# Banded attention with the keys' low part blanked out to 128 rows for each group

## The chip, the cores and the metric

The kernel runs on one core of one Trainium2 chip. The metric is the device time of the whole kernel in microseconds. A profile is one execution, recorded instruction by instruction.

## The reference, cut to what matters

The reference is two transformer blocks. The part that the change touches is the banded attention of the first block (two layers), over 1024 latent tokens and 256 context tokens, with six query heads in two groups that share keys and values:

```
def block(args):                       # 128 queries, each sees 256 context keys and a band of up to 384
    i, q_b = args
    start = i * Q_BLOCK
    k_b = lax.dynamic_slice_in_dim(kp, start, band, axis=1)
    v_b = lax.dynamic_slice_in_dim(vp, start, band, axis=1)
    q_pos = start + q_off
    k_pos = start - SWA_WINDOW + k_off
    valid = (jnp.abs(q_pos[:, None] - k_pos[None, :]) <= SWA_WINDOW) & ((k_pos >= 0) & (k_pos < s_len))[None, :]
    s_loc = jnp.einsum('bqgrd,bkgd->bgrqk', q_b, k_b).astype(jnp.float32) * SWA_SCALE
    s_loc = jnp.where(valid, s_loc, -jnp.inf)
    s_ctx = jnp.einsum('bqgrd,bcgd->bgrqc', q_b, k_ctx).astype(jnp.float32) * SWA_SCALE
    p = sink_softmax(jnp.concatenate([s_ctx, s_loc], axis=-1), sink).astype(v.dtype)
    return (jnp.einsum('bgrqc,bcgd->bqgrd', p[..., :n_ctx], v_ctx)
            + jnp.einsum('bgrqk,bkgd->bqgrd', p[..., n_ctx:], v_b))
```

Layer 0 also lets the 256 context tokens attend to themselves. The head dimension is 64. Everything is float32.

## The kernel before, in words

The program is a row of stages; each is a block in which every engine has its own instruction stream, and at its end all engines meet in a barrier. `window_attention` is one such stage and runs twice, for layer 0 (with context tokens) and for layer 1 (without). It has no DMA and, before the change, nothing on GpSimd except the clearing of semaphores.

The work is cut into units: one block of 128 queries and one of six heads. Layer 0 has 2 context blocks and 8 latent blocks, so 60 units; layer 1 has 8 latent blocks, 48 units. Context units see 2 tiles of 128 keys, the units of the first and last latent block 4, and all others 5.

The score products are made in a fast format of float32 that keeps only a high part. So queries and keys are each split into a high and a low part. `keys` holds, for each of the two groups, the keys' high part twice: in rows 0 to 63 and again in rows 64 to 127. `qs` holds, for a group, the queries' high part in the group's own 64 rows (`half(g)`) and the low part in the other 64. One matmul with the 128-row tile `q2` over `keys` therefore gives high times high plus low times high. The remaining term, the queries' high part times the keys' low part, is a second matmul (L982) with the 64-row tile `q1`, over `klo`, where both groups share one tile of 128 rows, 64 rows each. Both add into the same bank of PSUM. Masks of the band are added by a matmul of a bf16 identity with a bf16 mask (L984).

TensorE's order is written out by hand: scores of units 0 and 1, and then for each unit u the transposes of its probabilities (`turned`, L993), the scores of unit u + 2 (L981, L982, L984), and the products with the values (`products`, L1003 and L1010). The other engines follow by semaphores:

- ScalarE splits off the high parts (L1031 keys, L1039 queries, once per block), takes the exponentials (L1047, and L1051 for the sink), and copies the first four transposed tiles back (L1064).
- VectorE makes the low parts (L1078 keys, L1085 queries), the row maximum (L1092) and its scaling (L1093), copies the fifth transposed tile (L1119), and makes reciprocal (L1100) and output (L1102). In the loop its order for unit u is: fifth tile of u, maximum of u + 2, output of u - 1, and once in six units the queries of the next block.

The first scores wait for `k_lo` and `q_lo`. `products(u)` waits for the output of u - 2 (`o_out`), the sink's exponential and the copies of the transposed tiles.

Of the kernel before, what the change touches and what calls it, by code (L numbers as in the profile page):

```python
# [8 lines left out]
F32 = mybir.dt.float32  # L9
# [12 lines left out]
NT = NCTX + NLAT  # L22
# [528 lines left out]
class Scaled:  # L551
# [65 lines left out]
    def link(self, dve):  # L617
        if self.linked is None:
            self.linked = Links(dve, self.own)
        return self.linked  # L620
# [214 lines left out]
CKV, KR, SK, SVT, CQ, SQ, CB, CC, CU = 0, 1, 2, 3, 4, 6, 9, 11, 13  # L835
# [86 lines left out]
def window_attention(k, l, with_ctx):  # L922
# [6 lines left out]
    PR, MIX, SV = k.at(PR0, 15, NT), k.at(HT0, KD, NT), k.at(SV0, NT // P * 2, P)  # L929
# [1 line left out]
    prev, nxt, idb = (k.bmask[:, n * P:(n + 1) * P] for n in range(3))  # L931
    NB, H = NLAT // P, 6
    o = XT0
    keys, klo = k.part(o, 2, NT), k.part(o + 2 * NT, NT)
    o += 3 * NT
    qs = [k.part(o + 6 * P * g, 2, 3, P) for g in range(2)]
    o += 12 * P
    sinks, es = k.at(o, H, P), k.at(o + H * P, 2, P)
# [13 lines left out]
    half = lambda g: slice(64 * g, 64 * g + 64)  # L952

    with k.stage() as (block, sem):
        k_hi, k_lo, q_hi, q_lo, s_full, nb_set, p_set, sk_set, own = [sem() for _ in range(9)]
        t_full, pt_a, pt_b, pv_done, r_set, o_out = [sem() for _ in range(6)]
        pieces = ([(0, NCTX), (NCTX, NLAT)] if with_ctx else [(0, NT)])
        piece = lambda u: 2 if units[u][0] and with_ctx else 1

        @block.tensor  # L960
        def _(pe):
            def scores(u):
                kind, b, h = units[u]
                g, f, n = h % 2, h // 2, u // H
                if h == 0:
                    pe.wait_ge(k_lo, 2 * piece(u))
                    pe.wait_ge(q_lo, 2 * n + 2)
                if u >= 2:
                    pe.wait_ge(p_set, u - 1)
                S = k.psum[:, 1024 * (u % 2):1024 * (u % 2) + 1024]  # L970
                q2, q1 = qs[g][:, n % 2, f, :], qs[g][half(g), n % 2, f, :]
                todo = [(0, 0, NCTX, [])]
                if kind:
                    t = band(b)
                    masks = {b - 1: prev, b + 1: nxt}
                    todo += [(NCTX, NCTX + P * t[0], 2 * P, t[:2])]
                    if len(t) > 2:
                        todo += [(512, NCTX + P * t[2], P, t[2:])]
                for c0, k0, n_, ts in todo:
                    hide = [(c0 + P * x, masks[y]) for x, y in enumerate(ts) if y in masks]  # L980
                    pe.matmul(S[:, c0:c0 + n_], q2, keys[:, g, k0:k0 + n_], start=True, stop=False, skip_group_check=True)  # L981
                    mm = pe.matmul(S[:, c0:c0 + n_], q1, klo[half(g), k0:k0 + n_], start=False, stop=not hide, skip_group_check=True)  # L982
                    for c1, mask in hide:
                        mm = pe.matmul(S[:, c1:c1 + P], idb, mask, start=False, stop=True, skip_group_check=True)  # L984
                mm.then_inc(s_full, 1)

            def turned(u):
                pe.wait_ge(p_set, u + 1)
                if u:
                    pe.wait_ge(pt_a, u)  # L990
                    pe.wait_ge(pt_b, second(u)) if second(u) else None
                for t in range(tiles(u)):
                    mm = pe.transpose(k.bank[4 + t // 4][:, (t % 4) * P:(t % 4 + 1) * P], pr[:, u % 2, t * P:(t + 1) * P], k.ident[:, :])  # L993
                    if t == min(4, tiles(u)) - 1 or t == 4:
                        mm.then_inc(t_full, 1)

            def products(u):
                kind, b, h = units[u]
                if u >= 2:
                    pe.wait_ge(o_out, u - 1)  # L1000
                pe.wait_ge(sk_set, u + 1)
                out = k.bank[6 + u % 2][:, 0:P]
                pe.matmul(out, es[:, u % 2, :], k.ident[:, :], start=True, stop=False)  # L1003
                for t in range(tiles(u)):
                    if t == 0:
                        pe.wait_ge(pt_a, u + 1)
                    if t == 4:
                        pe.wait_ge(pt_b, second(u + 1))
                    tile = t if t < CT else CT + band(b)[t - CT]
                    mm = pe.matmul(out, SV[:, 2 * tile + h % 2, :], pt[:, u % 2, t, :], start=False, stop=(t == tiles(u) - 1))  # L1010
                mm.then_inc(pv_done, 1)

            scores(0)
            scores(1)
            for u in range(N):
                turned(u)
                if u + 2 < N:
                    scores(u + 2)
                products(u)

        def count_t(u):

            return u + second(u)

        @block.scalar
        def _(act):
# [43 lines left out]
        @block.vector  # L1070
        def _(dve):
            link = Links(dve, own)

            def keys_of(n):
                t0, nt = pieces[n]
                for g in range(2):
                    dve.wait_ge(k_hi, 2 * n + g + 1)
                    dve.tensor_tensor(klo[half(g), t0:t0 + nt], PR[half(g), SK, t0:t0 + nt], keys[half(g), g, t0:t0 + nt].bitcast(F32),  # L1078
                                      ALU.subtract).then_inc(k_lo, 1)

            def queries(n):
                t0 = tokens(*blocks[n])
                for g in range(2):
                    dve.wait_ge(q_hi, 2 * n + g + 1)
                    dve.tensor_tensor(qs[g][half(1 - g), n % 2, :, :], PR[half(g), SQ:SQ + 3, t0:t0 + P],  # L1085
                                      qs[g][half(g), n % 2, :, :].bitcast(F32), ALU.subtract).then_inc(q_lo, 1)

            def maxima(u):
                h = units[u][2]
                dve.wait_ge(s_full, u + 1)  # L1090
                n = tiles(u) * P
                link(dve.reduce_max(mx[:, u:u + 1], k.psum[:, 1024 * (u % 2):1024 * (u % 2) + n], AX.X))  # L1092
                dve.tensor_scalar(nb[:, u:u + 1], mx[:, u:u + 1], -SWA_SCALE, sink[:, h:h + 1], ALU.mult, ALU.min).then_inc(nb_set, 1)  # L1093

            def outputs(u):
                kind, b, h = units[u]
                t0 = tokens(kind, b)
                out = k.bank[6 + u % 2]
                dve.wait_ge(pv_done, u + 1)
                dve.reciprocal(rec[0:64, u % 2, :], out[64:P, 0:P]).then_inc(r_set, 1)  # L1100
                dve.wait_ge(r_set, u + 1)
                dve.tensor_tensor(MIX[half(h % 2), 3 + h // 2, t0:t0 + P], out[0:64, 0:P], rec[0:64, u % 2, :], ALU.mult).then_inc(o_out, 1)  # L1102

            queries(0)
            keys_of(0)
            link(dve.memset(sinks[:, :, 0:64], -1e30))
            for h in range(H):
                link(dve.tensor_scalar(sinks[:, h, 64:P], k.ones[:, 0:64], sink[:, h:h + 1], -1.0, ALU.mult, ALU.mult))
            maxima(0)
            queries(1)  # L1110
            if len(pieces) > 1:
                keys_of(1)
            maxima(1)
            for u in range(N):
                if tiles(u) > 4:
                    dve.wait_ge(t_full, count_t(u) + 2)
                    if u >= 2:
                        dve.wait_ge(pv_done, u - 1)
                    dve.tensor_copy(pt[:, u % 2, 4, :], k.bank[5][:, 0:P]).then_inc(pt_b, 1)  # L1119
                if u + 2 < N:  # L1120
                    maxima(u + 2)
                if u:
                    outputs(u - 1)
                if u % H == 2 and 2 <= u // H + 1 < len(blocks):
                    queries(u // H + 1)
            outputs(N - 1)
# [693 lines left out]
def first_half(k, l):  # L1820

    with_ctx = l < LAYERS - 1
    project_in(k, l, with_ctx)
    window_attention(k, l, with_ctx)
    latent_projections(k, l, with_ctx)
    latent_attention(k, l, with_ctx)
    mixed(k, l, with_ctx)
    return lambda kt, t0: k.gain[:, (2 * l + 1) * KD + kt, (1 if t0 < NCTX else 0):(2 if t0 < NCTX else 1)]
# [1845 lines left out]
```

## Time and profile before

| | us |
|---|---|
| median of three runs | 4456.78 (4451.52 to 4461.4) |
| span of the profiled execution | 4445.8 |
| stage in layer 0, from the first scores on | 203.31 |
| stage in layer 1, from the first scores on | 174.31 |

The profiled execution has a span of 4445.8 us from its first to its last instruction; its own total time is not listed beside it, so the span stands against the runs, whose median is 11.0 us above. PE is TensorE's matmul, PEld its weight load, DVE VectorE, ACT ScalarE, POOL GpSimd, SP the queue that issues DMAs. PEclk is the share of TensorE's full clock that was granted. The end of a matmul in the trace is modelled and includes its latency, so matmuls overlap in the records; the distance between starts tells the pace. L982 is line 982 of the kernel.

### The profile page before, as it was taken

To read this page: it belongs to the slowest core of one execution; us is meant where nothing else is said; L and a number is where in the kernel's file an instruction comes from. 1 tells how busy PE (TensorE), PEld (TensorE's weight loads), DVE (VectorE), ACT (ScalarE), POOL (GpSimd) and SP (SyncE) were. 2 spreads that over 40 slices of the span, in tenths; PEclk is the share of its full clock that TensorE was granted. 3 is DMA by queue.
4 is the path that set the end of the run, shared out by engine and by line. 5 is a ranking of instruction groups with operands and counts; after the bars stand their busy time and mean duration, and the time that the engine had idled before them with its cause. 6 is when DMAs were issued, how large, how long until landed. Compare 5 with 4: busy or idle time off the path is not lost. (4 is left out here: it accounts for less than half of the span.)

```text
span 4445.8 us, 51677 instructions
## 1 busy us (share of the span) xinstructions
PE 4031.7 (91%) x20694; PEld 3142.7 (71%) x20694; DVE 2167.2 (49%) x3353; ACT 1301.5 (29%) x2259; POOL 506.4 (11%) x597
## 2 busy tenths in 40 slices
PE   7989999897999979898988799799976999998997
PEld 5878655664777769785656699677744778887875
DVE  3577655423111155676553433475565365554444
ACT  3234533222111132344333233311344211112232
POOL 1000111102212210002111111200102100000011
PEclk8999999997999989998999899899887999999999
DMA  6000000337766641000012799312001211112111
GB/s 247 33 20 1 16 1 1 139 155 314 260 249 236 210 173 39 15 1 16 1 67 107 273 337 346 106 48 86 21 1 53 76 43 48 48 48 82 50 57 57
DMA packets 73878, 453.30 MB, mean 102 GB/s; under 512 B 8000, under 2 KB 12624, under 8 KB 57680
## 3 DMA queue, kind: packets, MB, share of 16 engines
q1 hardware_dynamic: 56960, 389.73, 23.2%
q0 software_dynamic: 13088, 47.19, 3.9%
q10 hardware_dynamic: 3632, 13.63, 0.8%
q8 instruction: 138, 2.26, 0.2%
q14 instruction: 60, 0.49, 0.0%
HBM read 394.95 MB, written 55.57 MB: 101 GB/s over the span
## 5 line engine op out<-in xcount | busy, mean ns | idle before, releaser
L2290 PEld LDWEIGHTS psum<-words,words 128*128 128x128 f32 x4096 | 514.6, 192 | 10.4 <-issue 9.1
L2290 PE MATMUL psum<-words,words 128*128 128x160 f32 (+1 forms) x4096 | 515.9, 289 | 1.4 <-DVE words L392 0.9
L675 PE MATMUL psum<-words,words 128*128 128x512 f32 x1104 | 440.6, 399 | 32.3 <-DVE words L715 27.9
L676 PE MATMUL psum<-words,words 128*128 128x512 f32 x1104 | 441.6, 400 | 0.0
L677 PE MATMUL psum<-words,words 128*128 128x512 f32 x1104 | 436.8, 396 | 0.0
L1605 PE MATMUL psum<-words,words 128*128 128x428 f32 (+1 forms) x720 | 253.2, 352 | 29.4 <-DVE words L1698 29.4
L675 PEld LDWEIGHTS psum<-words,words 128*128 128x128 f32 x1104 | 210.9, 191 | 86.3 <-DVE words L715 29.4
L1317 PE MATMUL psum<-words 128*128 128x512 f32 (+1 forms) x504 | 255.1, 588 | 0.0
L1606 PE MATMUL psum<-words,words 128*128 128x428 f32 (+1 forms) x720 | 249.9, 347 | 0.0
L1607 PE MATMUL psum<-words,words 128*128 128x428 f32 (+1 forms) x720 | 249.1, 346 | 0.0
L677 PEld LDWEIGHTS psum<-words,words 128*128 128x128 f32 x1104 | 209.8, 190 | 48.4
L676 PEld LDWEIGHTS psum<-words,words 128*128 128x128 f32 x1104 | 209.9, 190 | 46.9 <-issue 1.0
L694 ACT ACTIVATE words<-words 128x1024 fp32r<-128x1024 f32 x69 | 73.1, 1060 | 579.8 <-DMA words<-in_w_up 379.3
L1361 ACT ACTIVATE words<-psum 128x512 f32<-128x512 f32 (+1 forms) x252 | 147.7, 586 | 293.5 <-PE psum L1309 293.5
L1389 DVE TENSOR_REDUCE words<-psum 128x1 f32<-128x512 f32 (+1 forms) x300 | 163.3, 587 | 143.9 <-PE psum L1287 143.1
L792 PE MATMUL psum<-words,words 128*128 128x512 f32 (+1 forms) x448 | 173.9, 388 | 33.6 <-DVE words L515 33.3
L1307 PE MATMUL psum<-words,words 97*128 97x512 f32 (+1 forms) x252 | 191.9, 761 | 4.2 <-ACT words L1348 4.2
L591 POOL TENSOR_TENSOR words<-words 128x512 f32<-128x512 f32 (+1 forms) x56 | 76.1, 1391 | 1017.0 <-ACT words L584 1017.0
L2387 DVE TENSOR_TENSOR words<-words,psum 128x160 f32<-128x160 f32 x64 | 20.6, 322 | 319.0 <-ACT words L2350 319.0
L794 PE MATMUL psum<-words,words 128*128 128x512 f32 (+1 forms) x448 | 172.0, 384 | 0.0
L793 PE MATMUL psum<-words,words 128*128 128x512 f32 (+1 forms) x448 | 171.6, 383 | 0.0
L1605 PEld LDWEIGHTS psum<-words,words 128*128 128x128 f32 x720 | 137.8, 191 | 34.6 <-DVE words L1698 29.7
(436 smaller groups left out, 7986.8 us busy)
## 6 DMA issues: line engine op xcount, KB each, us to landing
words<-in_w_gate SPq DMA_DIRECT2D x32, 2048.0 KB, 8.0
words<-in_w_up SPq DMA_DIRECT2D x32, 2048.0 KB, 12.5
words<-in_w_down SPq DMA_DIRECT2D x32, 2048.0 KB, 12.9
words<-in_ada_w SPq DMA_DIRECT2D x24, 2048.0 KB, 14.6
words<-in_w_in SPq DMA_DIRECT2D x55, 512.0 KB, 3.4
words<-in_w_up SPq DMA_DIRECT2D x44, 512.0 KB, 3.4
words<-in_w_down SPq DMA_DIRECT2D x44, 256.0 KB, 2.6
words<-in_x SPq DMA_DIRECT2D x2, 5120.0 KB, 22.5
```

The source lines that it names most:

```text
L675: pe.matmul(out, hi[:, j, w], S.parts[0](kt, t0, nt), start=(kt == 0), stop=False)
L676: pe.matmul(out, hi[:, j, w], S.parts[1](kt, t0, nt), start=False, stop=False)
L677: mm = pe.matmul(out, lo[:, j, w], S.parts[0](kt, t0, nt), start=False, stop=(kt == KD - 1))
L792: pe.matmul(out, hi[:, j, w], x[0](kt, t0, n), start=(kt == 0), stop=False)
L793: pe.matmul(out, hi[:, j, w], x[1](kt, t0, n), start=False, stop=False)
L794: mm = pe.matmul(out, lo[:, j, w], x[0](kt, t0, n), start=False, stop=(kt == KT - 1))
L1307: pe.matmul(to, k_hi[0:ROW + 1, h % 2, key], q_hi[0:ROW + 1, h % 2, t0:t0 + n], start=True, stop=False)
L1317: pe.matmul(k.bank[O_BANK[u % 2]][:, 0:n], V[:, 6 * t + h, :], pt[:, x % R, 0:n], start=(t == 0), stop=(t == keys - 1)).then_inc(d_done, 1)
L1605: pe.matmul(out, whi[:, j, w], xhi[:, kt, c0:c0 + nc], start=(kt == 0), stop=False)
L1606: pe.matmul(out, whi[:, j, w], xlo[:, kt, c0:c0 + nc], start=False, stop=False)
L1607: mm = pe.matmul(out, wlo[:, j, w], xhi[:, kt, c0:c0 + nc], start=False, stop=(kt == KD - 1))
L2290: mm = pe.matmul(k.bank[m % 2][:, u * W:(u + 1) * W], ring[:, side[j], w0:w0 + P], xgT[:, j, kt, 0:W], start=(kt == 0), stop=(kt == KD - 1))
```

## The change

The low part of the keys gets a tile of its own for each group, all 128 rows high. The group's rows hold the low part as before, the other 64 rows are set to zero by GpSimd at the start of the stage. The second score matmul then takes the same 128-row stationary tile `q2` as the first. Its zero rows cancel the queries' low part. TensorE waits for both memsets before its first scores.

```
-    keys, klo = k.part(o, 2, NT), k.part(o + 2 * NT, NT)
-    o += 3 * NT
+    keys, klo = k.part(o, 2, NT), k.part(o + 2 * NT, 2, NT)
+    o += 4 * NT
...
-        t_full, pt_a, pt_b, pv_done, r_set, o_out = [sem() for _ in range(6)]
+        t_full, pt_a, pt_b, pv_done, r_set, o_out, blank = [sem() for _ in range(7)]
...
                 if h == 0:
+                    if n == 0:
+                        pe.wait_ge(blank, 2)
                     pe.wait_ge(k_lo, 2 * piece(u))
                     pe.wait_ge(q_lo, 2 * n + 2)
...
-                q2, q1 = qs[g][:, n % 2, f, :], qs[g][half(g), n % 2, f, :]
+                q2 = qs[g][:, n % 2, f, :]
...
-                    mm = pe.matmul(S[:, c0:c0 + n_], q1, klo[half(g), k0:k0 + n_], start=False, stop=not hide, skip_group_check=True)
+                    mm = pe.matmul(S[:, c0:c0 + n_], q2, klo[:, g, k0:k0 + n_], start=False, stop=not hide, skip_group_check=True)
...
+        @block.gpsimd
+        def _(pool):
+            for g in range(2):
+                pool.memset(klo[half(1 - g), g, :].bitcast(F32), 0.0).then_inc(blank, 1)
...
-                    dve.tensor_tensor(klo[half(g), t0:t0 + nt], PR[half(g), SK, t0:t0 + nt], keys[half(g), g, t0:t0 + nt].bitcast(F32),
+                    dve.tensor_tensor(klo[half(g), g, t0:t0 + nt], PR[half(g), SK, t0:t0 + nt], keys[half(g), g, t0:t0 + nt].bitcast(F32),
                                       ALU.subtract).then_inc(k_lo, 1)
```

## Rows read from the trace of the kernel before

**Rows 1.** The page, part 1: busy time, share of the span, instructions.
```profile
PE 4031.7 (91%) x20694; PEld 3142.7 (71%) x20694; DVE 2167.2 (49%) x3353; ACT 1301.5 (29%) x2259; POOL 506.4 (11%) x597
```

**Rows 2.** Windows: length, busy us (count) by engine, PEclk, DMA share, GB/s.
```profile
300.89:504.20 203.31, 193.01 (x1248) 157.44 (x1248) 151.72 (x303) 101.06 (x203) 0.00 (x0) 0.95 0.00 1
1835.89:2010.20 174.31, 171.76 (x1128) 140.31 (x1128) 125.25 (x249) 81.19 (x157) 0.00 (x0) 0.97 0.00 1
```

**Rows 3.** The line L982: duration ns min/median/max, first and last start, forms.
```profile
L982 PEld LDWEIGHTS psum<-words,words x276: 182/183/286, 301.4 to 2002.3; 64*128 64x128 f32 x138
```

**Rows 4.** Timeline of PE, an interior unit: start us, duration us, line, shapes, count.
```profile
403.35 0.36 PE L981 MATMUL psum<-words,words 128*128 128x256 f32 x1
403.64 0.38 PE L982 MATMUL psum<-words,words 64*128 64x256 f32 x1
403.95 0.38 PE L981 MATMUL psum<-words,words 128*128 128x256 f32 x1
404.26 0.38 PE L982 MATMUL psum<-words,words 64*128 64x256 f32 x1
404.58 0.23 PE L984 MATMUL psum<-bmask 128*128 128x128 bf16 x1
404.62 0.31 PE L981 MATMUL psum<-words,words 128*128 128x128 f32 x1
404.86 0.32 PE L982 MATMUL psum<-words,words 64*128 64x128 f32 x1
...
405.18 0.44 PE L1003 MATMUL psum<-ident,words 128*128 128x128 f32 x2
405.45 1.28 PE L1010 MATMUL psum<-words 128*128 128x128 f32 x10
406.57 0.71 PE L993 MATMUL psum<-ident,words 128*128 128x128 f32 x5
407.03 0.36 PE L981 MATMUL psum<-words,words 128*128 128x256 f32 x1
```

**Rows 5.** Timeline of DVE, the same stretch; idle time before and releaser in brackets.
```profile
401.69 0.82 DVE L1092 TENSOR_REDUCE words<-psum 128x1 f32<-128x640 f32 x1 [1.10 <-PE psum L984]
402.55 0.21 DVE L1093 TENSOR_SCALAR words<-words,negsink 128x1 f32<-128x1 f32 x1
402.80 0.96 DVE L1100 RECIPROCAL words<-psum 64x128 f32<-64x128 f32 x1
403.79 0.28 DVE L1102 TENSOR_TENSOR words<-psum,words 64x128 f32<-64x128 f32 x1
404.11 0.29 DVE L1119 COPY words<-psum 128x128 f32<-128x128 f32 x1
```

**Rows 6.** Timeline of ACT, the same stretch.
```profile
403.52 0.60 ACT L1064 ACTIVATE words<-psum 128x512 f32<-128x512 f32 x1 [2.11 <-PE psum L993]
```

**Rows 7.** Timeline of PE and its weight loads, end of the stage before layer 0's.
```profile
290.12 0.36 PE L1607 MATMUL psum<-words,words 128*128 128x426 f32 x1
290.12 0.19 PEld L1605 LDWEIGHTS psum<-words,words 128*128 128x128 f32 x1
290.32 0.36 PE L1605 MATMUL psum<-words,words 128*128 128x426 f32 x1
```

**Rows 8.** Lines, 285 to 520 us: busy us, mean ns, idle before, releaser.
```profile
L1085 DVE TENSOR_TENSOR words<-words,words 64x384 fp32r<-64x384 f32 x20 | 11.0, 549 | 1.2 <-ACT words L1039 0.9
```

**Rows 9.** Timeline of PE, a context unit.
```profile
320.28 0.49 PE L1003 MATMUL psum<-ident,words 128*128 128x128 f32 x2 [0.31 <-DVE words L1102]
```

**Rows 10.** Lines of POOL over the whole span: its memset of 1280 columns.
```profile
L1622 POOL MEMSET words<- 128x1280 f32 x2 | 2.4, 1197 | 0.0
```

**Rows 11.** Timeline of DVE and PE at the start of the stage in layer 0.
```profile
295.15 2.08 DVE L1792 TENSOR_TENSOR words<-words 128x1280 f32<-128x1280 f32 x1 [1.70 <-ACT words L1647]
...
300.89 0.58 PE L981 MATMUL psum<-words,words 128*128 128x256 f32 x1 [8.07 <-DVE words L1078]
```

**Rows 12.** Windows, two microseconds at the first edge units of layer 0.
```profile
332.00:334.00 2.00, 2.00 (x9) 1.55 (x7) 1.08 (x2) 0.89 (x3) 0.00 (x0) 0.50 0.00 0
```

## The prediction

> **What bounds the kernel now.** I read the page first: TensorE (PE) is busy for 91% of the span, VectorE (DVE) for 49% [rows 1]. That is an average over many stages, so the question belongs to the two stages that the change touches. The windows table shows them: 203.31 us in layer 0 and 174.31 us in layer 1, together 8.5% of the span, with PE busy for 95% and 98.5% of them, DVE for 75% and 72%, and the DMA queues idle [rows 2]. No transfer can hide or hold anything here. One line of the score product takes 276 matmuls over both stages [rows 3]; the code gives the same number (12 for the context units, 132 for the latent units of each layer).
>
> Next comes the timeline of one unit. I call a unit *interior* when its block has both neighbours (blocks 1 to 6: 6 x 6 heads x 2 layers = 72 units), *edge* for blocks 0 and 7 (24), and *context* (12, layer 0 only). An interior unit on PE is five transposes (L993), the scores of the unit two ahead (L981, L982, L984), and the products (L1003, L1010). From one L981 to the next unit's first L981 it is 407.03 - 403.35 = 3.68 us, with no gap on PE [rows 4]. DVE sat idle for 1.10 us in the same unit, waiting for the masks' matmul L984 [rows 5]. ScalarE waits for L993 for 2.11 us [rows 6]. So PE sets the pace of an interior unit and both others wait for it.
>
> The reader is to see how unevenly PE's 3.68 us are spent. The transposes take 407.03 - 406.57 = 0.46, that is 0.092 each. The sink product and the ten L1010 matmuls take 406.57 - 405.18 = 1.39; the ten alone 0.112 each. The eight score instructions take 405.18 - 403.35 = 1.83, although most stream only 256 or 128 columns [rows 4]. Each 256-column score matmul is followed after 0.29 to 0.32 us, where 256 columns at the full clock of 2.4 GHz are 0.107 us. What is left, 0.18 to 0.21, is the length of one weight load (median 0.183 for the 64-row tile, [rows 3]). In this stretch each load waits until the matmul ahead has streamed.
>
> It is not so between tiles of the same 128 rows. In the stage before, L1605 to L1607 stream 426 columns each with a new 128x128 tile for each, and follow each other at 0.20 us, when 426 columns alone are 0.178; the 0.19 us load of the next tile lies wholly beside the running matmul [rows 7]. L1010 does the same at 0.112 us, and the mask L984 (128 rows) is followed by L981 (128 rows) after 0.04 [rows 4]. The pairs that are slow are those in which the tile goes from 128 rows to 64 or back, in both directions. There are six such turns in an interior unit, four in an edge unit, two in a context unit.
>
> **The change part by part.** *Tile of the low product.* L982 takes all 128 rows. It streams as many columns as before into the same bank; the blank half adds zeros. It still loads its weights (nothing skips a repeated tile), so no instruction disappears. What goes is the exposure of the loads. My price for a 256-column pair member is its streaming 0.107 plus the 0.017 to 0.02 that L1605 shows over its own, 0.125; for a 128-column one 0.112, as L1010; for a mask 0.045. Scores of an interior unit: 4 x 0.125 + 2 x 0.112 + 2 x 0.045 = 0.81. The bounds: if loads remain exposed, 1.83 as now; if loads are hidden but one cannot start until the previous load record of 0.19 has ended, 6 x 0.19 + 2 x 0.045 = 1.23. L1010's 0.112 speaks against the latter, so I take 0.81. PE's unit becomes 0.46 + 0.81 + 1.39 = 2.66, so 1.02 less.
>
> *What is late next.* PE cannot use all of this. DVE does, for each unit, the maximum (0.82), its scaling (0.21), reciprocal (0.96), product (0.28) and the copy of the fifth tile (0.29): from 401.69 to 404.11 + 0.29 = 404.40, 2.71 us, and 0.03 to the next [rows 5]. On top of that it splits the queries once per block, two of 0.549 [rows 8], with gaps 1.17 us, or 0.195 per unit. DVE's unit is 2.74 + 0.19 = 2.93, longer than PE's 2.66. So the interior unit falls from 3.68 to 2.93, and DVE is the new bound. The loop that runs over both engines (scores, maximum, outputs of the unit before, then the products two on) takes over two units 0.27 + 2.38 on DVE, 0.06 back, and 1.39 + 0.46 + 0.75 on PE, 5.31, or 2.66 each: under DVE's own 2.74, but close. ScalarE's copy L1064 ends at 404.12 [rows 6]; its first reader L1010 would come at about 403.35 + 0.81 + 0.27 = 404.43, 0.3 later. It stays hidden. Gain: 72 x (3.68 - 2.93) = 54 us.
>
> *Edge units.* They lack a 128-column pair and its mask (0.53), one transpose (0.09) and two L1010 (0.22): 3.68 - 0.84 = 2.84 now. Their scores go from 1.30 to 4 x 0.125 + 0.045 = 0.55, PE's unit to 2.09. DVE's is 2.74 less the copy (0.32) and a maximum over 512 instead of 640 columns (0.14): 2.28, with half of the queries 2.38. Gain 0.46. The last two units of each stage have no scores beside them, so 20 to 22 count: 9 us.
>
> *Context units.* PE already waits for DVE's L1102 before L1003, 0.31 us [rows 9]. Nothing is gained. The first scores of each stage, before DVE has anything to do, are sooner by some 1 us: 2 us together.
>
> *The blank half.* GpSimd sets two pieces of 64 x 1280, priced by its memset of as many elements per partition, 1.197 us each [rows 10]: 2.4 us. The first scores wait for DVE's L1078 until 300.89 anyway, with PE idle 8.07 us [rows 11]. The last instruction of the stage before on DVE ends at 297.23 [rows 11]; with half a microsecond for the barrier GpSimd would be done near 300.2, about 0.7 early. If it starts 1.7 us later it costs 1 us in layer 0; in layer 1 the first L1078 splits 1280 columns instead of 256, so the wait is longer and the blank is free. GpSimd has no other work in this stage, and nobody is queued behind it. On PE the wait holds all that follows, but it stands before a wait that is longer. I take 0, at worst 2. The subtraction L1078 only writes to another place. The klo tile grows by 1280 words, and later tiles move; no shared bytes arise, so no wait.
>
> **The sum.** 54 + 9 + 2 = 65 us. A second route from DVE's busy time gives a ceiling: layer 1 has 125.25 us in 249 instructions, at 0.03 between them 132.7, against 174.31: at most 41.6; layer 0 has 151.72 + 9.1 = 160.8 against 203.31: at most 42.5 [rows 2]. From both come start, end and the context's waits, in which DVE must be idle, some 6 and 10 us. That leaves 35 + 32 = 67. The stages are closed by barriers on all engines, so what they lose, the whole loses. The profiled span is 4445.8; 4445.8 - 65 = 4380.8. The median of the three runs, 4456.78, is 11.0 above that span; I carry these over: 4391.8, rounded to 4392.
>
> **The rivals.** *The engines mesh worse (0.13).* The two-engine loop was only 0.08 below DVE's own, the queries' burst hits both ScalarE and DVE, and a load may cost 0.19. With a unit of 3.1 to 3.3 the interior gain is 72 x 0.48 = 35 and with edges about 42: 4415 us. For it: the margins above; against it: in the context units DVE-paced work already runs with PE waiting only 0.31 [rows 9].
>
> *Same tile, no overlap (0.08): the change does not do what it says.* If the exposed load came from something else in this pair, e.g. that both write the same bank, the unit stays 3.68, and 276 loads go from 0.183 to the 0.19 of a 128-row tile (2 us), the blank 0 to 2: 4457 to 4461. Against it: L1605 to L1607 write one bank, and L984 to L981 too, and neither shows the exposure [rows 4, 7]. The Trainium skill's page "TensorE: Matmul & The Clock Gate", section "The mechanism" of Part 3, says that a weight load overlaps a running matmul only when its row group differs; by that rule the changed kernel, with equal row groups throughout, would hide nothing, and the time would stay at 4457. The trace does not agree: 128-row loads lie beside 128-row matmuls at 0.20 us spacing [rows 7]. The skill's page "TensorEngine Tiling (Array Packing)", section "Key Properties", says the opposite way round that a change of tiling mode drains the engine, which would give the 4392.
>
> *The clock falls (0.04), the other side.* In the context-to-latent turn the granted clock stands at 0.50, the 1.2 GHz level, for some us [rows 12], after PE had been waiting for DVE. In the new stretch PE waits in every unit: 2.66 of 2.93. At half clock the unit is at most 2 x 2.66 = 5.3. The gain of 65 is used up once 65 / (5.3 - 2.93) = 27 of 72 interior units run so; with all of them the time is 4392 + 171 = 4563, with half 4477. Against it: the same columns go through PE in 2.93 instead of 3.68 us, so it works denser than now.
>
> **How the numbers follow.** The forecast (loads hidden, DVE bound, gain 55 to 75) gets 0.75, and its own range is 4382 to 4402. The 0.2% that can be told from no change is 9 us. Range for 8 in 10: from 4380 (a gain a little above the ceiling) to 4416, which takes in the meshing rival. Faster: 0.75 + 0.13 = 0.88; within 0.2%: 0.08; slower: 0.04.
>
> **What would show it.** L982's loads and matmuls appear as 128*128. L981 to L982 starts come at about 0.125 us. L1003 in interior units is preceded by idle time released by DVE's L1102, DVE's idle before L1092 goes from 1.1 us to nearly nothing, and reciprocals come at 2.7 us with one of 3.9 in six. The stages are near 170 and 139 us. Wrong would be: spacing still 0.31 (rival two), DVE idle left in each unit (rival one), a clock under 0.95 in these windows (rival three), or a first L981 later than 301 with GpSimd as releaser.

## The result, and the profile after

The changed kernel takes 4384.97 us (median of four runs, 4382.16 to 4388.44) against 4454.15 before. The ratio is 0.9841, with a 95% interval of 0.9827 to 0.9855: 1.6% faster. A second set of five runs of the same kernel gave 4385.59 against 4452.22, ratio 0.9849 (0.9835 to 0.9863). The forecast was 4392, with 4380 to 4416 as its range.

The page and the windows show where it went. TensorE is 87 us less busy in the whole span [rows 1]; the two stages, counted from the first score matmul, go from 203.31 to 166.21 and from 174.31 to 139.09 us [rows 2]. From the first instruction of a stage to the first one of the next they fall from 389.3 to 317.2 us together, 72.2 less. The instruction counts of PE and VectorE are as before.

First the page of the changed kernel, part 1, then two windows of it (length, busy us and count for PE, PEld, DVE, ACT, POOL, then PEclk, DMA share, GB/s):

```profile
PE 3945.0 (90%) x20694; PEld 3104.4 (71%) x20694; DVE 2162.8 (49%) x3353; ACT 1302.3 (30%) x2259; POOL 513.3 (12%) x601
```

```profile
301.00:467.21 166.21, 148.59 (x1248) 141.51 (x1248) 150.37 (x303) 101.15 (x203) 0.00 (x0) 0.97 0.00 1
1798.37:1937.46 139.09, 132.46 (x1128) 127.71 (x1128) 124.17 (x249) 81.25 (x157) 0.00 (x0) 0.97 0.01 1
```

PE is now idle for 18 us of the first window, VectorE for 16, each with the small gaps between its instructions. Before, PE was idle for 10 and VectorE for 52 of a longer stretch. Line numbers shift by two to seven: L981 is now L983, L982 is L984, L984 is L986, L993 is L995, L1003 is L1005, L1010 is L1012, L1078 is L1085, L1092 is L1099, L1100 is L1107, L1102 is L1109, L1119 is L1126.

The line of the low product in the changed kernel (duration min/median/max), to set beside [rows 3]:

```profile
L984 PEld LDWEIGHTS psum<-words,words x276: 187/192/337, 301.2 to 1929.7; 128*128 128x128 f32 x138
```

All 276 loads are still there and each is 9 ns longer than the 64-row ones. The gain is not in them but in where they lie. In the kernel before, the load for L982 starts only when the matmul ahead (L981, at 403.35) has streamed, 0.29 us after it and at the same time as the record of its own matmul [rows 4]:

```profile
403.64 0.18 PEld L982 LDWEIGHTS psum<-words,words 64*128 64x128 f32 x1
```

In the changed kernel the same load starts at 403.27, 0.08 us after the start of the matmul ahead (403.19) and 0.12 before its own (403.39), so it runs while the one ahead streams:

```profile
403.16 0.19 PEld L983 LDWEIGHTS psum<-words,words 128*128 128x128 f32 x1
403.27 0.19 PEld L984 LDWEIGHTS psum<-words,words 128*128 128x128 f32 x1
```

This is PE's timeline of the changed kernel, one interior unit, to set beside [rows 4]:

```profile
403.19 0.36 PE L983 MATMUL psum<-words,words 128*128 128x256 f32 x1
403.39 0.28 PE L984 MATMUL psum<-words,words 128*128 128x256 f32 x1
403.51 0.28 PE L983 MATMUL psum<-words,words 128*128 128x256 f32 x1
403.63 0.28 PE L984 MATMUL psum<-words,words 128*128 128x256 f32 x1
403.75 0.23 PE L986 MATMUL psum<-bmask 128*128 128x128 bf16 x1
403.79 0.30 PE L983 MATMUL psum<-words,words 128*128 128x128 f32 x1
403.93 0.28 PE L984 MATMUL psum<-words,words 128*128 128x128 f32 x1
404.05 0.23 PE L986 MATMUL psum<-bmask 128*128 128x128 bf16 x1
404.11 0.44 PE L1005 MATMUL psum<-ident,words 128*128 128x128 f32 x2
404.39 1.28 PE L1012 MATMUL psum<-words 128*128 128x128 f32 x10
405.51 0.71 PE L995 MATMUL psum<-ident,words 128*128 128x128 f32 x5
405.97 0.36 PE L983 MATMUL psum<-words,words 128*128 128x256 f32 x1
```

The scores take 404.11 - 403.19 = 0.92 us where they took 1.83. The products (1.40) and the transposes (0.46) are unchanged. A 256-column score matmul is followed after 0.12 us instead of 0.31. The unit is 405.97 - 403.19 = 2.78.

That is a unit in which nothing disturbs. Across a whole block there is a pattern of six, which the reciprocals of the changed kernel's VectorE timeline show (idle time and releaser in brackets):

```profile
407.10 0.82 DVE L1099 TENSOR_REDUCE words<-psum 128x1 f32<-128x640 f32 x1 [0.20 <-PE psum L986]
...
408.20 0.96 DVE L1107 RECIPROCAL words<-psum 64x128 f32<-64x128 f32 x1
...
409.40 1.13 DVE L1092 TENSOR_TENSOR words<-words,words 64x384 fp32r<-64x384 f32 x2
...
411.75 0.96 DVE L1107 RECIPROCAL words<-psum 64x128 f32<-64x128 f32 x1
...
414.23 0.96 DVE L1107 RECIPROCAL words<-psum 64x128 f32<-64x128 f32 x1
...
416.11 0.82 DVE L1099 TENSOR_REDUCE words<-psum 128x1 f32<-128x640 f32 x1 [0.27 <-PE psum L986]
...
417.21 0.96 DVE L1107 RECIPROCAL words<-psum 64x128 f32<-64x128 f32 x1
```

The distances are 3.55, 2.48 and 2.98 us, and then three times 2.78: 17.36 us for six units, a mean of 2.89. In the first of them VectorE splits the queries, 1.13 us; in this unit and the next one VectorE does not wait at all. PE waits once in the six units, behind the split, for VectorE's output (PE and VectorE of the changed kernel):

```profile
412.74 0.28 DVE L1109 TENSOR_TENSOR words<-psum,words 64x128 f32<-64x128 f32 x1
412.95 0.27 DVE L1126 COPY words<-psum 128x128 f32<-128x128 f32 x1
413.08 0.49 PE L1005 MATMUL psum<-ident,words 128*128 128x128 f32 x2 [0.41 <-DVE words L1109]
413.15 0.81 DVE L1099 TENSOR_REDUCE words<-psum 128x1 f32<-128x640 f32 x1
```

PE's unit is 3.41 us there and 2.78 to 2.82 in the five others. VectorE's recorded waits in the six units are 0.27, 0.20 and 0.20 us, so its own work is at most 17.36 - 0.67 = 16.7 us. PE's own is 6 x 2.78 = 16.7 as well. The waits of the changed kernel from 301 to 467 us (total us, times, longest) name both directions; most of the first row lies in the context and edge units:

```profile
PE psum L1005 <- DVE words L1109: 10.2, 19, 1.1
...
DVE words L1099 <- PE psum L986: 4.6, 19, 0.5
```

In the same view of the kernel before, VectorE's wait for the masks was 39.3 us in 40 waits; it is 4.6 us now.

### The profile page after: what moved, and what is told of

Read it like the earlier page. It is cut to its first block and busy times, and to the rows that moved or that the text cites. A ratio compares the mean times of both kernels' runs of the same rounds, so it can differ in the third digit from the quotient of the medians.

```text
span 4380.3 us, 51681 instructions
## 1 busy us (share of the span) xinstructions
PE 3945.0 (90%) x20694; PEld 3104.4 (71%) x20694; DVE 2162.8 (49%) x3353; ACT 1302.3 (30%) x2259; POOL 513.3 (12%) x601
```

## The experiments

Three questions: is it the turn between tile heights that exposes a load, and what does one turn cost; what stops the gain at 2.89 us per unit; and is the blank half hidden. Unit times below are distances of reciprocals in layer 0; "stages" is the length of both stages together, from one stage's first instruction to the next one's.

**Grouped order.** On the kernel before, all tiles as they were:

```
                 for c0, k0, n_, ts in todo:
-                    hide = [(c0 + P * x, masks[y]) for x, y in enumerate(ts) if y in masks]
                     pe.matmul(S[:, c0:c0 + n_], q2, keys[:, g, k0:k0 + n_], start=True, stop=False, skip_group_check=True)
-                    mm = pe.matmul(S[:, c0:c0 + n_], q1, klo[half(g), k0:k0 + n_], start=False, stop=not hide, skip_group_check=True)
-                    for c1, mask in hide:
-                        mm = pe.matmul(S[:, c1:c1 + P], idb, mask, start=False, stop=True, skip_group_check=True)
+                for c0, k0, n_, ts in todo:
+                    for c1, mask in [(c0 + P * x, masks[y]) for x, y in enumerate(ts) if y in masks]:
+                        pe.matmul(S[:, c1:c1 + P], idb, mask, start=False, stop=False, skip_group_check=True)
+                for c0, k0, n_, ts in todo:
+                    mm = pe.matmul(S[:, c0:c0 + n_], q1, klo[half(g), k0:k0 + n_], start=False, stop=True, skip_group_check=True)
```

> The kernel before, with the score instructions of a unit in another order: all high products (128 rows), then the masks (128 rows), then all low products (64 rows). Same instructions, same tiles, two turns between 128 and 64 rows per unit instead of six (interior) or four (edge). Theory (a turn of tile height exposes the next weight load, a load between tiles of one height is hidden): an interior unit goes from 3.68 us to 3.08 to 3.16 us, the time falls by about 45 us, to some 4409. Rival (every load of a 64-row tile, and the one behind it, is exposed, whatever stood before): only two of six exposures go, the unit stays near 3.3 and the time near 4424. Second rival (the exposure comes from the low product right behind the high one in the same place of PSUM): the unit falls to about 2.8 to 2.9 and the time to some 4388.

In this form the opening flag of a bank's second product leaves the high product of the context keys out; the last experiment of this group has it in. It took 4398.42 us, ratio 0.9884 (0.9868 to 0.9901). Its PE timeline:

```profile
404.43 0.54 PE L980 MATMUL psum<-words,words 128*128 128x256 f32 x3
404.81 0.29 PE L983 MATMUL psum<-bmask 128*128 128x128 bf16 x2
405.03 0.56 PE L985 MATMUL psum<-words,words 64*128 64x256 f32 x3
405.51 0.49 PE L1004 MATMUL psum<-ident,words 128*128 128x128 f32 x2
405.84 1.28 PE L1011 MATMUL psum<-words 128*128 128x128 f32 x10
406.95 0.71 PE L994 MATMUL psum<-ident,words 128*128 128x128 f32 x5
407.42 0.36 PE L980 MATMUL psum<-words,words 128*128 128x256 f32 x1
```

The 64-row products now stand together: the three of them and the turn behind them take 0.48 us, the three 128-row ones 0.38. The plain unit is 2.99 us, below the 3.08 to 3.16 of the theory and far from the 3.3 of the rival that blames the 64-row tile itself. It lies 0.21 above the changed kernel's 2.78, for two turns. The time is 11 us below the 4409 of the theory: a turn costs less than was assumed. The second rival, the place in PSUM, forecast 2.8 to 2.9 and 4388, and the measured unit lies halfway between it and the theory. It is the changed kernel that speaks against this rival: there the low product still comes right behind the high one in the same place of PSUM, and follows it after 0.12 us.

> The grouped order once more for a second look at its unit: again 2.99 us for a plain interior unit, and a span within 5 us of the first.

This was the same kernel once more: 2.99 us again and a span of 4394.9 against 4398.9.

> The grouped order on the kernel before once more, with the flag that opens a PSUM bank set only on the first product of each bank, so that all terms are kept. Theory: the flag costs nothing, so the two stages take 332 us together as in the first grouped run (before 389, changed kernel 317), and the time is about 4397. It says what the order of the instructions alone can bring, without the blanked half: 57 of the 72 us. Rival (the first grouped run was short because of how the bank was opened): above 340 us for the stages.

```
-  q2, keys[:, g, k0:k0 + n_], start=True, stop=False
+  q2, keys[:, g, k0:k0 + n_], start=(c0 % 512 == 0), stop=False
```

4391.0 us, ratio 0.9865 (0.9846 to 0.9883), stages 331.0. The stages came as expected (332), the time 6 us below the expected 4397; the stages don't explain that, and the rest of the span scatters by more (below). Reordering alone, with no blank half and no larger tile, brings 58 of the 72 us in the stages. In the medians of one chip it is 61 of 67 us: 4391.0 here, 4385.59 for the changed kernel.

**All score products on 64 rows.** The high product takes `q1` and `keys[half(g)]`, grouped, masks last:

```
-                    pe.matmul(S[:, c0:c0 + n_], q2, keys[:, g, k0:k0 + n_], start=True, stop=False, skip_group_check=True)
+                    pe.matmul(S[:, c0:c0 + n_], q1, keys[half(g), g, k0:k0 + n_], start=True, stop=False, skip_group_check=True)
```

> The kernel before, with all score products on the 64-row tile and the masks last. It leaves out the queries' low part times the keys' high part. As many matmuls and columns as before, two turns per unit. Theory: the loads between 64-row tiles are hidden as well, so an interior unit takes 3.05 to 3.2 us, as in the grouped order, some 4409 in all. Rival (the 64-row tile itself exposes its load): the unit stays at 3.5 to 3.7 us, 4440 to 4457.

Like the first grouped form, this kernel also leaves out the high product of the context keys, by the opening flag of the bank's second product. It took 4398.25 us, ratio 0.9893 (0.9876 to 0.9909), plain unit 2.99 to 3.00, a little below the expected 3.05. Its PE timeline:

```profile
403.50 0.57 PE L980 MATMUL psum<-words,words 64*128 64x256 f32 x3
403.91 0.51 PE L982 MATMUL psum<-words,words 64*128 64x256 f32 x3
404.35 0.29 PE L985 MATMUL psum<-bmask 128*128 128x128 bf16 x2
```

The three high products (256, 256 and 128 columns) take 0.41 us, from 403.50 to 403.91; in the kernel before they take 0.29, 0.31 and 0.24 [rows 4]. A tile of 64 rows has its load hidden as long as its neighbours have 64 rows too. The height as such costs nothing.

**Masks on 64 rows.** The changed kernel, with turns put back where no score product changes:

```
-                        mm = pe.matmul(S[:, c1:c1 + P], idb, mask, start=False, stop=True, skip_group_check=True)
+                        mm = pe.matmul(S[:, c1:c1 + P], idb[0:64, :], mask[0:64, :], start=False, stop=True, skip_group_check=True)
```

> The changed kernel, with the mask matmuls cut to 64 rows of identity and mask (half of the mask is left out). This puts four turns of height back into an interior unit (two into most edge units) without touching the score products. Theory: the interior unit goes from a mean of 2.90 back to 3.4 to 3.55 us, the time rises by 40 to 55 us, to about 4430. Rival (the gain was a matter of the pair of score products alone, or of the layout of the low part): no change, 4385.

4408.8 us, ratio to before 0.9912 (0.9895 to 0.9928), stages 342.9 against 317.2. Its PE timeline around the two masks:

```profile
403.19 0.28 PE L984 MATMUL psum<-words,words 128*128 128x256 f32 x1
403.40 0.23 PE L986 MATMUL psum<-bmask 64*128 64x128 bf16 x1
403.56 0.33 PE L983 MATMUL psum<-words,words 128*128 128x128 f32 x1
403.72 0.28 PE L984 MATMUL psum<-words,words 128*128 128x128 f32 x1
403.93 0.23 PE L986 MATMUL psum<-bmask 64*128 64x128 bf16 x1
404.09 0.49 PE L1005 MATMUL psum<-ident,words 128*128 128x128 f32 x2
```

The direction is the theory's: the same score products, and 26 us lost in the stages. So neither the pair of products nor the new layout of the low part made the gain. The size was too high in the expectation: the plain unit rose to 3.24, not 3.4 to 3.55, and the time to 4408.8, not about 4430. Four turns cost 0.46 us, 0.11 to 0.12 each. At the first mask it is 0.09 on the way in (0.21 after L984 instead of 0.12) and 0.12 on the way out (0.16 instead of 0.04). The load of such a mask is itself only 0.09 us long, and it starts with its matmul, as the load at a turn did in the kernel before:

```profile
403.40 0.09 PEld L986 LDWEIGHTS psum<-bmask 64*128 64x128 bf16 x1
```

**One group only.** The changed kernel with the 64-row low product for the second group:

```
-                    mm = pe.matmul(S[:, c0:c0 + n_], q2, klo[:, g, k0:k0 + n_], start=False, stop=not hide, skip_group_check=True)
+                    rw = slice(0, P) if g == 0 else half(g)
+                    mm = pe.matmul(S[:, c0:c0 + n_], qs[g][rw, n % 2, f, :], klo[rw, g, k0:k0 + n_], start=False, stop=not hide, skip_group_check=True)
```

> The changed kernel with the 128-row tile for the first group's heads only; the second group's low product stays at 64 rows. Half of the turns are back. Theory with PE as the bound of the slow units: units alternate between 2.78 and 3.68 us of PE work, mean 3.23, which lies above VectorE's 2.93; the time is about 4415, so 39 of the 69 us remain. If VectorE did not cap the full change, halving the turns would halve the gain: 4420.

4417.05 us, ratio 0.9931 (0.9915 to 0.9948), stages 348.5. The units alternate, 3.68 and 2.79 us. Between the forecast of 4415 and the 4420 of a straight line the runs do not decide: removing half of the turns gains 31 us in them, the full change 67 to 69, and the interval of 0.9915 to 0.9948 is 15 us wide. The stages do decide. The first half of the turns gains 389.3 - 348.5 = 40.8 us there, the second half 348.5 - 317.2 = 31.3, where a straight line would be 36 each; 2 to 3 us of the first half are the granted clock in the profile of before (below), which leaves the order as it is. So the gain flattens as the theory said. In this kernel the slow units leave VectorE room for the split of the queries, and no pattern of six appears; in the changed kernel it does, at 0.11 us per unit.

**What stops it.** The split of the queries goes from VectorE to GpSimd, for blocks 2 and up:

```
+            for n in range(2, len(blocks)):
+                t0 = tokens(*blocks[n])
+                for g in range(2):
+                    pool.wait_ge(q_hi, 2 * n + g + 1)
+                    pool.tensor_tensor(qs[g][half(1 - g), n % 2, :, :], PR[half(g), SQ:SQ + 3, t0:t0 + P],
+                                       qs[g][half(g), n % 2, :, :].bitcast(F32), ALU.subtract).then_inc(q_lo, 1)
...
-                if u % H == 2 and 2 <= u // H + 1 < len(blocks):
-                    queries(u // H + 1)
             outputs(N - 1)
```

> The changed kernel, with the queries' low part of blocks 2 and up made by GpSimd instead of VectorE. Theory (in the changed kernel VectorE's own work, 17.4 us for six interior units with one split of the queries, is what TensorE's 6 x 2.785 = 16.7 us runs into): the pattern 3.54, 2.49, 2.98 us goes and all interior units take 2.78 to 2.8, so 72 x (2.90 - 2.79) = 8 us less, some 9 with the edge units: about 4376 against 4385 for the changed kernel, or 73 us below the kernel before of this call. Rival (TensorE alone is the bound and the pattern averages out): no change against the changed kernel. Rival (GpSimd's longer subtraction holds the block's first scores): slower by some us.

> The kernel before with the same move of the queries' split from VectorE to GpSimd. Theory: VectorE had about 1 us idle in each of its units, so the interior unit stays at 3.68 us and the time within 0.1% of before. Rival (VectorE's work was already part of the pace before the change): some us faster.

> The changed kernel as it is, beside the one with the queries' split on GpSimd, on one chip. Theory: some 66 to 72 us below before; stages 317 us together.

> The changed kernel with the queries' split on GpSimd, again, now beside the changed kernel. Theory: stages 308 us together, so 9 us less than the changed kernel, 4372 to 4377 where that has 4382 to 4386. If the first run's larger distance (86 us below before) was more than scatter, the distance to the changed kernel is 15 us or more, and something outside the two stages has moved.

| | us, median | ratio to before | stages | unit |
|---|---|---|---|---|
| changed kernel, again | 4385.59 | 0.9849 (0.9835 to 0.9863) | 317.7 | 2.78, with 3.54, 2.49, 2.98 |
| changed kernel, split on GpSimd | 4364.75 | 0.9807 (0.9794 to 0.9820) | 307.9 | 2.78 |
| the same, again | 4372.09 | 0.9817 (0.9803 to 0.9830) | 307.7 | 2.79 |
| kernel before, split on GpSimd | 4451.58 | 1.0000 (0.9991 to 1.0009) | 388.1 | 3.68 |

The move is worth nothing on the kernel before (1.2 us less in the stages, which an episode of the granted clock in the profile of before can explain, below) and 9 to 10 us in the stages on the changed one. So the rival that TensorE alone is the bound fails, and so does the one that GpSimd's subtraction holds the scores. The theory had the size right, but its 17.4 us are not VectorE's own work: 0.7 of them are its waits. What holds the changed kernel is that two engines with 16.7 us of work each wait for one another once per block. The work moved is the same; what changed is whose work sets the pace. With it the pattern of six is gone. The VectorE timeline of the repeated run shows equal units, with VectorE still a little early:

```profile
400.03 0.96 DVE L1113 RECIPROCAL words<-psum 64x128 f32<-64x128 f32 x1
...
402.81 0.96 DVE L1113 RECIPROCAL words<-psum 64x128 f32<-64x128 f32 x1
...
404.49 0.82 DVE L1105 TENSOR_REDUCE words<-psum 128x1 f32<-128x640 f32 x1 [0.21 <-PE psum L986]
```

Beside the changed kernel on the same chip the runs differ by 13.5 us, the spans of the profiled executions by 8.0 and the stages by 10.1. So the expectation of 9 holds for the stages; the runs' larger distance is not explained by them. The rest of the span differs from one execution to the next by as much (below), which makes scatter likely, but this is not shown. The first run lies 11 us under its expected 4376, the second within its 4372 to 4377. It is the fastest kernel of the study, 1.8 to 1.9% under before.

**The blank half.** Each piece is set twice, one after the other, and TensorE waits for all four:

```
-  for g in range(2):
+  for i, g in enumerate((0, 1, 0, 1)):
+      if i >= 2:
+          pool.wait_ge(blank, i)
```

> The changed kernel with every piece of the low part blanked twice, one after the other, before TensorE may start. Theory: in layer 0 the blanks end at 302.7 to 303.0 instead of 300.4, so the first scores start 1.8 to 2.1 us later than 301.0, released by GpSimd; in layer 1, where the subtraction of the keys is done 7 us after the stage starts, the first scores do not move. The whole is within noise of the changed kernel. Rival (the blank is on the path already): both stages start their scores 2.4 us later.

Start of the stage in layer 0, changed kernel:

```profile
297.68 1.07 ACT L1046 ACTIVATE words<-words 64x384 fp32r<-64x384 f32 x2 [2.47 <-PEq L138]
297.99 2.37 POOL L1030 MEMSET words<- 64x1280 f32 x2 [2.01 <-SPq L138]
...
301.04 0.55 PE L983 MATMUL psum<-words,words 128*128 128x256 f32 x1 [8.12 <-DVE words L1085]
```

The same with the blank doubled:

```profile
299.40 1.07 ACT L1048 ACTIVATE words<-words 64x384 fp32r<-64x384 f32 x2 [2.47 <-PEq L138]
299.71 4.85 POOL L1032 MEMSET words<- 64x1280 f32 x4 [2.01 <-SPq L138]
...
304.62 0.58 PE L983 MATMUL psum<-words,words 128*128 128x256 f32 x1 [9.99 <-POOL words L1032]
```

In the changed kernel the blanks end at 300.36, 0.7 us before the first scores. Doubled, they hold the first scores for 1.86 us more (5.22 after the stage's start instead of 3.36), as expected, and not at all in layer 1. Yet the stage in layer 0 is 169.86 us long against 169.88. This is one execution, of 4383.76 us, beside 4385 for the changed kernel. ScalarE takes its first exponential only after it has split the latent keys, so TensorE waits there anyway: 5.5 us in the changed kernel. The blank is hidden twice over: a start 1.7 us later, which I had priced at 1 us in layer 0, would have cost nothing.

## Why the prediction was right

*The exposed load.* Right in mechanism: loads are hidden between tiles of one height and exposed at a turn. Four kernels show it from different sides: two turns instead of six (2.99), 64 rows throughout (2.99), turns brought back by the masks alone (3.24), half of them back (3.68 and 2.79 in turn). The changed kernel has the same row groups throughout and hides its loads between score products. So the rule that I had weighed as a rival, that of the Trainium skill's page "TensorE: Matmul & The Clock Gate", section "The mechanism", that a load overlaps a running matmul only when its row group differs, does not hold here: the load at 403.27 runs beside a matmul of the same 128 rows. The same section of the Trainium skill also lets a load into the background weight buffer go ahead, and the trace does not speak against that. The Trainium skill's page "TensorEngine Tiling (Array Packing)", section "Key Properties", says that a change of tiling mode drains TensorE; this agrees with all four, and with the load at 403.64 that starts only behind the matmul ahead.

One argument against the rival of the shared bank was misread: of L984 and the L981 behind it the first writes columns 256 to 383 of the scores and the second 512 to 639, which are two banks. L1605 to L1607 do write one bank, and the changed kernel's own pairs settle it. One thing was not tried: a turn from one 64-row half to the other, since within a unit all 64-row tiles lie in the same half.

*The price of PE's scores.* I took 0.81, it is 0.92. The 256-column matmuls are cheaper than assumed (0.12, not 0.125), but the first one behind the transposes takes 0.20, and the 128-column ones take 0.14 and 0.12, not 0.112. Most likely the load of the first has its turn behind those of the transposes, which stream too few columns to hide it. The rows fit: its load starts at 403.16, 0.03 before its matmul, while the next one's starts 0.12 before. No run separated this. So PE's unit is 2.78 and not 2.66.

*VectorE as the next bound.* Right that VectorE stops the gain, wrong in how, and the number came out by luck. I had VectorE late in every unit with 2.93 us of work, and PE waiting each time with 2.66. Measured are at most 16.7 us for six units, 2.78 each, and PE's own is 2.78 too. My 2.71 without the queries came from one of two kinds of unit that alternate: in [rows 5] the copy of the fifth tile starts 0.32 us behind the product, in the other kind 0.21 behind. Where VectorE runs without a wait in the shorter kind, a unit takes 2.48 (411.75 to 414.23); the mean without the queries is about (16.7 - 1.05) / 6 = 2.6, with 1.05 for the split. So VectorE was priced 0.15 too high and PE 0.12 too low. The pace of 2.89 is above both: the split comes in one piece, and PE then waits once per block and loses nearly 0.7 us (17.36 against 16.7). That is a small form of the rival "the engines mesh worse", whose 3.1 to 3.3 did not come. The sign that I had named, an idle PE before L1003 in all interior units, shows in one of six, and the reciprocals come at 2.78 with one 3.55, one 2.48 and one 2.98, not at 2.7 with one 3.9. The separate run shows that the splits alone are worth 9 to 10 us.

*The terms.* Interior units: 72 x (3.68 - 2.89) = 57 us, 54 forecast. The 54 were near because two errors nearly cancel: VectorE's 0.15 too much, and the 0.11 per unit that the burst costs, which I had left out. Edge and context units, starts and ends: 72 - 57 = 15 us, where I had 11. Edge units run at 2.35 instead of 2.83, as forecast with 2.38. A large part of the surplus is the granted clock: in the kernel before it stood at 0.50 after the context units [rows 12], and in this execution of the changed kernel it stays at 1.00 there. The window of the changed kernel over the first edge units:

```profile
331.00:333.00 2.00, 1.55 (x14) 1.45 (x13) 1.87 (x5) 0.88 (x3) 0.00 (x0) 1.00 0.00 0
```

Two units took 4.21 and 3.75 us there before, and take 2.28 and 2.15 now. But this is not the change's doing: with the split on GpSimd the kernel before, whose score products are the same, had the granted clock at 1.00 from 331 to 333 us, and its two units took 2.28 and 2.65. So some 2 to 3 us of the 72 are an episode of the profiled execution of the kernel before. The rival with the clock did not come.

*The sum.* The forecast span was 4380.8, the measured one 4380.3, and this is closer than the working deserves. The stages gave 72 instead of 65; the rest of the span is 4063.1 us against 4056.5 before. Over the profiled executions of this study that rest lies between 4056 and 4072, for kernels that are alike in it, so before's was at the low end. A larger gain in the stages and a longer rest met by chance. And the 11.0 us that I added from span to runs was scatter: the changed kernel's profiled run is 4382.16 for a span of 4380.3, so only 1.9 lies around it. Against medians, 69.2 and 66.6 us are gained and 65 were forecast.

## What to carry to other kernels

Look in TensorE's timeline at the distance of starts across every change of tile height: if it exceeds the columns by about the length of a load, either give the small product the full height (blank rows are free to stream) or put the products of one height together. Here 256 columns followed each other after 0.12 us at 64 rows and at 128. The second needs no larger tile, only that a bank is opened once, and already brought 58 of 72 us in the stages here. After such a gain work out the sum of the next engine over a whole block, with its once-per-block instructions included, from more than one unit. And where two engines have nearly the same sum, reckon with a loss at each burst: what was harmless while VectorE waited a microsecond per unit was worth 9 us here once it no longer did.

## What the runs showed of the hardware that I had not expected

- A turn does not cost a whole load of 0.18 to 0.19 us everywhere. It cost about 0.19 between two 256-column matmuls (0.31 instead of 0.12), 0.10 to 0.13 behind a 128-column one, and 0.09 into and 0.12 out of a 64-row bf16 mask, whose own load is 0.09 long.
- At the 1.2 GHz level (granted clock 0.50) a turn costs more: 256-column matmuls followed each other after 0.51 us in the kernel before (333.22, 333.73, 334.24) and after 0.21 in the changed kernel (301.39, 301.60, 301.81).
- A 64-row tile between 64-row tiles loads as hidden as a 128-row tile between 128-row tiles.
- GpSimd's subtraction of two 64 x 384 pieces took 2.07 us where VectorE's took 1.13, and VectorE's own times were unchanged beside it (reciprocal 0.96, product 0.28).
